# Reordering the waits of a two-block network kernel: loads, filters, attention norm, merges and norms

## What is computed

```python
# block 1
m = silu(c) @ w_ada + b_ada                       # shifts, scales, gates
h = rmsnorm(x) * (1 + sc1) + sh1;  z = h @ w_in + b_in
f = sin-MLP(t) @ f4 * decay                       # Hyena filters, 2 orders, fwd and bwd
f = f / sum(|f|)                                  # over time and direction
zc = short 3-tap convolution of z[:, :1536]; v, x1, x2 = split(zc)
for o in (0, 1): y = gate_o * (irfft(rfft(y) * rfft(f)[o]) + skip[o] * y)
q, k = rope(rmsnorm(z_q)), rope(rmsnorm(z_k))     # 8 heads of 64
na = softmax(q @ [k_window; rmsnorm(k_ctx)].T / 8 + bias) @ [v; v_ctx]
x += g1 * ((sig(z_g1) * (y @ w_hy_out) + sig(z_g2) * (na @ w_na_out)) @ w_out)
hf = rmsnorm(x) * (1 + sc2) + sh2
# PEER: 8 heads pick 16 of 16384 experts for each row by two-part keys
x += g2 * sum(softmax(best) * gelu(hf . u[idx]) * v[idx])
# block 2, two layers: attention and a state-space mixer (SSD) side by side,
h = rmsnorm(x);  merged = gates of (attention @ pa, y_ssd @ ps);  x += merged @ w_o
h = rmsnorm(x);  x += glu(conv(h @ w_up)) @ w_dn  # 22 column tiles
out = rmsnorm(x)
```

## Time and profile before

| | us |
|---|---|
| median of 3 runs (2389.24 to 2395.49) | 2389.31 |
| the profiled execution | 2386.79 |
| its span, first to last instruction | 2385.0 |
| TensorE busy (86%) | 2047.3 |
| VectorE (58%), ScalarE (42%), GpSimd (41%) | 1395.0, 994.6, 980.6 |

### The profile page before, as it was taken

How to read it: one execution, slowest core, us unless ns; L and a number is a source line. 1 busy time by engine, 2 the same in 40 slices (tenths; PEclk the granted TensorE clock), 3 DMA queues, 4 the chain that set the end, 5 groups by cost and what they waited for, 6 DMA issues and landing times.

```text
span 2385.0 us, 26693 instructions
## 1 busy us (share of the span) xinstructions
PE 2047.3 (86%) x9656; PEld 1505.9 (63%) x9656; DVE 1395.0 (58%) x2697; ACT 994.6 (42%) x1756; POOL 980.6 (41%) x562
## 2 busy tenths in 40 slices
PE   6898698778788777777799989989989988998998
PEld 1486467763333333333489777789978976777997
DVE  2785674466666676675336645257753673434776
ACT  1430334321212121211345677355554567744554
POOL 1162246554444444444377547610027844781000
PEclk9899799889989899899999999999989999998999
DMA  8141355459999999999655344445545533453552
GB/s 325 39 141 46 129 210 187 139 235 422 422 421 421 421 421 421 421 421 422 217 166 171 109 144 156 158 146 186 188 139 163 185 106 124 159 184 116 188 188 102
DMA packets 111012, 534.37 MB, mean 224 GB/s; under 512 B 12448, under 2 KB 12576, under 8 KB 77344
## 3 DMA queue, kind: packets, MB, share of 16 engines
q1 hardware_dynamic: 66960, 244.72, 31.1%
q0 software_dynamic: 38720, 275.96, 28.1%
q10 hardware_dynamic: 5200, 11.98, 1.6%
...
## 4 chain that ended last, share of the span: by engine, by line
PE 54%; DMA 24%; DVE 8%; ACT 7%; issue 4%; POOL 3%; ACTq 0%; DVEq 0%; SPq 0%; POOLq 0%
PE psum L791 53%; DMA pair_rows<-in_peer_uv,arena 10%; DMA arena<-in_peer_uv,arena 6%; DMA wring<-in_peer_uv,arena 5%; POOL w_lo L2369 2%; ACT w_hi L1251 2%; ACT arena L1262 1%; DVE arena L1619 1%; PE psum L839 1%; ACT arena L1510 1%; DMA wring<-in_w_ada 1%; ACT arena L1455 1%; DMA dve_junk<-acs_rows 1%; ACT a_hi L1258 1%; DVE dve_junk L1619 1%
## 5 line engine op out<-in xcount | busy, mean ns | idle before, releaser
L2369 POOL TENSOR_TENSOR w_lo<-wring,w_hi 128x1024 fp32r<-128x1024 f32 x282 | 697.9, 2489 | 729.7 <-ACT w_hi L1251 687.9
L1251 ACT ACTIVATE w_hi<-wring 128x1024 fp32r<-128x1024 f32 (+1 forms) x414 | 431.6, 1051 | 357.4 <-PE psum L791 311.7
L791 PE MATMUL psum<-w_hi,a_hi 128*128 128x512 f32 (+1 forms) x1056 | 425.1, 403 | 31.8 <-POOL w_lo L2369 20.7
L791 PE MATMUL psum<-w_lo,a_hi 128*128 128x512 f32 (+1 forms) x1056 | 415.5, 393 | 0.0
L791 PE MATMUL psum<-w_hi,a_lo 128*128 128x512 f32 (+1 forms) x1056 | 415.4, 393 | 0.0
L791 PE MATMUL psum<-arena 128*128 128x512 f32 (+7 forms) x1142 | 342.7, 458 | 81.9 <-ACT arena L1403 45.2
L791 PE MATMUL psum<-a_hi,w_hi 128*128 128x256 f32 x1312 | 377.7, 288 | 11.0 <-POOL w_lo L2369 3.8
L791 PE MATMUL psum<-a_lo,w_hi 128*128 128x256 f32 x1312 | 376.3, 287 | 0.0
L791 PE MATMUL psum<-a_hi,w_lo 128*128 128x256 f32 x1312 | 376.0, 287 | 0.0
L791 PEld LDWEIGHTS psum<-arena 128*128 128x128 f32 (+2 forms) x1142 | 186.5, 200 | 224.9 <-issue 159.0
L791 PE MATMUL psum<-pair_rows,arena 128*128 128x512 f32 x512 | 260.6, 663 | 67.3 <-ACT arena L1403 67.3
...
## 6 DMA issues: line engine op xcount, KB each, us to landing
wring<-in_w_up SPq DMA_DIRECT2D x88, 512.0 KB, 3.3
wring<-in_w_xbc SPq DMA_DIRECT2D x48, 512.0 KB, 3.3
wring<-in_w_dn SPq DMA_DIRECT2D x44, 512.0 KB, 3.3
wring<-in_w_adaT SPq DMA_DIRECT2D x32, 512.0 KB, 4.0
wring<-in_w_qkv SPq DMA_DIRECT2D x32, 512.0 KB, 3.5
wring<-in_w_z SPq DMA_DIRECT2D x32, 512.0 KB, 3.5
wring<-in_w_g SPq DMA_DIRECT2D x32, 512.0 KB, 3.4
wring<-in_w_ps SPq DMA_DIRECT2D x32, 512.0 KB, 3.3
```

The source lines that it names most:

```text
L791: mm = lambda o, a, b, start, stop: nc.tensor.matmul(o, a, b, start=start, stop=stop, skip_group_check=True)
L1251: a.reaches(A(w_hi[:, n % SPLIT_RING, 0:width], wring[:, c % RING, 0:width], ACT.Copy), hi_ready, n + 1)
L2369: nc.gpsimd.tensor_tensor(w_lo[:, r, 0:width], wring[:, c % RING, 0:width], w_hi[:, r, 0:width].bitcast(F32), ALU.subtract).then_inc(lo_re ...
```

## The change

1. **Loads in order of use.** The first four w_ada chunks go ahead of `consts`, x comes after all 16; on ScalarE's queue the first three filter matrices and `feats` go first, `f4` and the other tables after `ada(0)`; GpSimd loads the context after `ada` 1 is filled.
2. **Filters by order, their norm behind the DFT.** The filters of order 0 come first; sum and difference are made of filters that are not normalized; the sums follow the DFT, and VectorE multiplies the spectra by the reciprocal (`spectra_scaled`) during `zhy`. On ScalarE the norm of x and context comes ahead of the absolute values. The first `zhy` product waits for its inputs tile by tile.
3. **Short convolution from PSUM.** ScalarE takes the middle tap with scale and bias out of PSUM, VectorE adds the outer taps from PSUM.
4. **Attention norm.** Queries are normalized and rotated (in place, tables prepared early) behind order 0's spectrum products, keys behind order 1's; squares of projected rows are ScalarE's.
5. **Merge in halves.** `mT` is turned in two halves, the first ahead of the gate rows (block 2: in the middle of `ps` 2, 3), the second in the middle of `w_out` 0, 1 (`w_o` 0, 1). The eight late dots move from between `w_pq` chunks to `mix` and after `mT`.
6. **Norms by tile.** `norm_tiles` squares each half as its residual comes, with the root's table loaded ahead; scaling and output go by tile. The last two `dn` chunks are taken together in the order 0, 2, 1, 3. Transposed inputs are waited for singly (`ready`).
7. **GpSimd's low parts in two instructions** of half the width.

```diff
-    ada(3), add("filter", 8), g.append(("adaT", 3)), add("absum", 2)
+    ada(3), g.extend(("filter", i) for i in FILTER_ORDER), g.append(("adaT", 3))
     for o in range(2):
         g.extend([("dftf", 4 * o + i) for i in range(4)] + [("nyq", o)])
+    add("absum", 2)
     add("hT0", KD), add("hcT", KD)
     add("zhy", 12), add("zqkv", 2), add("vrow", 2)
     for o in range(2):
...
-    add("mix", 8), add("mT", KD), add("gb", 2), add("wout", 4)
-    add("hfT", KD), add("hfrow", 4), 
+    add("mix", 8), add("mT", 4), add("gb", 2), add("mT", 4, 4), add("wout", 4)
+    add("hfT", KD)
     for q in range(4):
-        g.extend([("pq", 4 * q + i) for i in range(4)] + [("ps", q)])
+        for i in range(4):
+            g.append(("pq", 4 * q + i))
+            if 4 * q + i == 0:
+                add("hfrow", 4)
...
+DOWN_ORDER = (0, 2, 1, 3)
+FILTER_ORDER = [4 * t + 2 * o + j for o in range(2) for t in range(TT) for j in range(2)]
 ADA_FIRST, ADA_DOTS, DOTS_PER_HEAD, LATE_DOTS = 4, 32, 3, 8
+LATE_AFTER = [("mix", 1), ("mix", 3), ("mix", 5), ("mix", 7)] + [("mT", KD - 1)] * 4
+LATE_AT = [2, 4, 6, 8, 9, 10, 11, 12]
...
+            if c == 4:
+                sp.dma_start(consts[:], d["consts"]).then_inc(S("consts_in"), 16)
+            if c == 4 * ADA_FIRST:
+                sp.dma_start(x[:], d["x"].rearrange("p (a b) -> p a b", b=D)).then_inc(S("x_in"), 16)
...
+        for i in FILTER_ORDER:
+            o = open_("filter", i)
+            t, j = i // 4, i % 4
+            close(mm(o, mlp_h[0:64, tile(t)], HW("f4")[0:64, j * 512:(j + 1) * 512], True, True))
         ada_columns(3)
...
-        pe.wait_ge(S("modulated_lo"), KD)
         for m_ in range(12):
-            feature_mm("w_in_hy", None, "zhy", m_)
+            feature_mm("w_in_hy", None, "zhy", m_, None if m_ else lambda k: pe.wait_ge(S("modulated_lo"), k + 1))
...
+        merged_turned("mT", merged, 0, 1)
         gate_rows("gb", 0, 1)
-        for c in range(2):
-            columns_of_rows("w_out", None, [("wout", 2 * c), ("wout", 2 * c + 1)], [0, 0])
-
-
-        pe.wait_ge(S("scaled"), 2)
+        columns_of_rows("w_out", None, [("wout", 0), ("wout", 1)], [0, 0], early=True,
+                        before=lambda: merged_turned("mT", merged, 1, 2), ready=lambda k: wait_read(pe, "mT", k))
...
+                feature_mm("w_pq", None, "pq", m_, None if m_ else lambda k: pe.wait_ge(S("modulated_lo"), 2 * KD + k + 1))
+                if m_ == 0:
+                    for t in range(TT):
+                        for half in range(2):
...
+            columns_of_rows("w2_ps", l, [(L + "ps", 0), (L + "ps", 1)], [0, 0], 8,
+                            ready=lambda k: wait_read(pe, L + "yT", k))
+            columns_of_rows("w2_ps", l, [(L + "ps", 2), (L + "ps", 3)], [0, 0], 8, early=True,
+                            before=lambda: merged_turned(L + "mT", merged2, 0, 3 + 2 * l))
+            columns_of_rows("w2_o", l, [(L + "wo", 0), (L + "wo", 1)], [0, 0], early=True,
+                            before=lambda: merged_turned(L + "mT", merged2, 1, 4 + 2 * l),
+                            ready=lambda k: wait_read(pe, L + "mT", k))
+            columns_of_rows("w2_o", l, [(L + "wo", 2), (L + "wo", 3)], [0, 0])
...
+                if c == FT // 2:
+                    pe.wait_ge(S("glu_ready"), FT * l + FT)
+                    last_two = [take("w2_dn", l), take("w2_dn", l)]
+                    for n in DOWN_ORDER:
+                        for k, w in zip((FT - 2, FT - 1), last_two):
+                            m = rows_mm(down[n], GLU_AT + k % GLU_RING, 1, n % 2, w, 512, False, k == FT - 1,
+                                        at=512 * (n // 2))
+                            if k == FT - 2 and n == 3:
+                                m.then_inc(weights_used, 1)
+                        close(m)
+                    break
                 for k in range(2 * c - 2, 2 * c) if c else ():
...
+        def norm_tiles(n, halves, ready):
+
+            a.done(A(lnw[:, 0:1], K("epscol"), ACT.Sqrt))
+            summed = []
+            for i in halves:
+                c, t = i // 2, i % 2
+                half = slice(512 * c, 512 * c + 512)
+                second = t in summed
+                ready(i)
+                part = ss[:, 2 + t:3 + t] if second else ss[:, t:t + 1]
+                a.done(A(xs[:, t, half], x[:, t, half], ACT.Square, accum_out=part))
+                a.settle()
+                if second:
+                    a.reaches(A(std[:, t:t + 1], part, ACT.Sqrt, scale=1.0 / D, bias=mean_half[:, t:t + 1]),
+                             S("tile_std"), 2 * n + t + 1)
+                else:
+                    a.done(A(mean_half[:, t:t + 1], part, ACT.Identity, scale=1.0 / D, bias=K("epscol")))
+                    summed.append(t)
+
...
+            a.reaches(A(zcT[:, m_, :], bank("zhy", m_)[:, 0:SEQ], ACT.Identity, bias=hy_bias[:, m_:m_ + 1],
+                        scale=V("cw", 12 + m_)), S("hy_first_tap"), m_ + 1)
...
+        def tiles_scaled(n):
+
+            for t in range(TT):
+                dve.wait_ge(S("tile_std"), 2 * n + t + 1)
+                v.done(T.reciprocal(rinv[:, t:t + 1], std[:, t:t + 1]))
+                v.settle()
+                v.reaches(T.tensor_scalar(xs[:, t, :], x[:, t, :], rinv[:, t:t + 1], None, ALU.mult),
+                         S("tile_scaled"), 2 * n + t + 1)
...
+        def spectra_scaled(o_):
+
+            wait_read(dve, "absum", o_)
+            v.done(T.reciprocal(rsum[:, o_, :], rsum[:, o_, :]))
+            v.settle()
+            for spectrum in (Kr[:, o_, :, :], Ki[:, o_, :, :]):
+                tt(spectrum, spectrum, rsum[:, o_:o_ + 1, :].to_broadcast([P, 2, 512]), ALU.mult)
+            tt(Kr0[:, o_, :], Kr0[:, o_, :], rsum[:, o_, :], ALU.mult)
...
+        filters_in(0)
+        even_and_odd(0)
+        filters_in(1)
+        ada_out(3)
+        even_and_odd(1)
+        absolutes(0)
+        absolutes(1)
...
+        def attention_queries():
+
+            dve.wait_ge(S("na_squares"), 2)
+            row_sums(na_sq, 0)
+            v.settle()
+            dve.sem_inc(S("na_sumsq"), 1)
+            roped_rows(0)
+            dve.wait_ge(S("na_std"), 1)
+            v.done(T.reciprocal(ninv[:, 0:16], nstd[:, 0:16]))
+            v.settle()
+            scaled_rows(qkv[:, :, 0:512], 0)
+            v.settle()
...
+            (attention_queries if o_ == 0 else attention_keys)()
...
+            late_dot("mix", n)
...
-                n = ADA_DOTS - LATE_DOTS + m_ // 2
-                ada_dots(n, n + 1)
...
-            nc.gpsimd.tensor_tensor(w_lo[:, r, 0:width], wring[:, c % RING, 0:width],
-                                    w_hi[:, r, 0:width].bitcast(F32), ALU.subtract).then_inc(lo_ready, 1)
+                pool.wait_ge(S("scaled"), 2)
+            half = width // 2
+            nc.gpsimd.tensor_tensor(w_lo[:, r, 0:half], wring[:, c % RING, 0:half],
+                                    w_hi[:, r, 0:half].bitcast(F32), ALU.subtract)
+            nc.gpsimd.tensor_tensor(w_lo[:, r, half:width], wring[:, c % RING, half:width],
```

523 lines of the change are left out of this document (284 added, 239 removed).

## The result

The changed kernel takes 2326.6 us (median of 4 runs, 2324.12 to 2328.98) against 2389.27 for the kernel before (4 runs, 2384.44 to 2395.49): ratio 0.974, 95% interval 0.972 to 0.976. It is faster by 62.7 us where 105 were forecast, and 2326.6 lies above the range of 2260 to 2312.

A forecast was written before the change was run, and what follows sets the result against it. TensorE was taken to bound the front and back parts, the DMA engines 507.33 to 1155 us. Terms of -75 up to the gather's start, -34 behind and +4 for halves made -105: 2284 us, range 2260 to 2312.

The forecast's parts named there:

- The attention and SSD sum: Attention and SSD stretches of two layers: +6.6 us, from +2.6 of the state-space part and all +4 of the halves.
- Merge and w_out: Merge to last w_out matmul: turning in halves removes a 4.4 us wait, moved dots delay two chunks; -0.6 us.
- Queries without dots: Query chunks up to the gather's first issue: without dots between them the gather starts at the last split; -20 us.
- The merge turned in halves: Each layer's merge behind the gather: turning in halves between chunks removes idle time and a low clock; -7 us per layer.
- Norm ahead of the FFN: In each layer, the 10.94 us norm stretch, of which TensorE works 3.69, shortens by 5 us.
- The tail: End of the kernel, 12.0 us with two full squares and a table load in it: -3.5 us.
- Loads -13: Kernel start: first w_ada chunk issued first lands at some 6 us instead of 19.4, other loads fit behind; -13.3 us.
- the loads are late: Rival, 8%: filter tables arrive late, decay products wait, 8 to 13 of the 13 us come back; 2292 to 2297.
- Filters -9.5, first projection -3.5: Filters ordered, norm behind the DFT: -9.5 us; first projection tile by tile, removing a 2.8 us wait and slow clock: -3.5.
- Halves +4: Every GpSimd low part in two instructions: extra launch shows only in GpSimd-paced places; +4 us (0 to +25).
- slower by halves: Rival, 3%: each extra GpSimd instruction costs 0.39 us beyond the 0.32 TensorE leaves free, making the kernel slower.
- the moved work meets GpSimd: Rival, 15%: keys late by 5, w_out late by 5, halves at +15; 2305 in the middle, 2314 at the far end.

The follow-up runs named there:

- e1: The changed kernel with each GpSimd low part as one instruction again instead of two halves: 2318.7 us, ratio 0.9708 to the kernel before.
- e2: The changed kernel with the eight late dots moved back between the query chunks: 2332.16 us, ratio 0.9767 to the kernel before.
- e4: The changed kernel with the first half of the merged rows turned after two ps chunks instead of four (second half likewise): 2315.35 us, ratio 0.9686.
- e5: The changed kernel with all 32 dots during the attention heads, four a head, none later: 2318.83 us, ratio 0.9739 to the kernel before.
- e9: e6 with x loaded four chunks later, the context after ada 3, and their waits behind the absolute values: 2323.93 us, ratio 0.9731.
- e11: e8 with the later x and context loads of e9: 2297.23 us, ratio 0.9619 to the kernel before.
- e12: e11 with low parts in halves in block 1 only, whole behind the gather: 2286.85 us, ratio 0.9596 to the kernel before.
- e3: The changed kernel with the twelve rotation-table products moved ahead of the short convolution: 2321.08 us, ratio 0.9731 to the kernel before.
- e6: e3 with ScalarE's norm of x and context also moved behind the absolute values: 2322.7 us, ratio 0.9733 to the kernel before.
- e7: The changed kernel with the edits of e4, e5 and e6 together: 2305.85 us, ratio 0.9665 to the kernel before.
- e8: e7 with each GpSimd low part as one whole instruction: 2300.01 us, ratio 0.9633 to the kernel before.
- e13: The kernel before with all dots in the attention heads, four a head, and low parts in halves: 2375.11 us, ratio 0.9949.

## Why the prediction was wrong

The direction and most mechanisms held: attention norm, second norm, the norm between the layers, and the first chunk at 5.99 us all within 0.5 us of their terms. The attention and SSD sum, +6.5 for +6.6, is luck: e1 with whole low parts has 375.0 there, the same as the kernel before, so the halves cost 6.5 of their own and the +2.6 booked beside them came to nothing. Of the signs that the prediction named, the first matmul at 6 us and the vanished wait at naT came, and the last w_pq split still releases the gather (0.28 us behind it); the DFT (51), the first score (213), the gather's start (432) and "no idle over 2 us at either mT" did not: 61, 226, 464 and 4.16.

The step that failed first is "Merge and w_out, -0.6 (-4 to +5)": +12.4, outside its own bounds. It named two mechanisms. The second, a read_low behind a dot, did not show: the 5.1 us wait for `a_lo` is ScalarE behind a late chunk. The first, a late slot, is the right one, but it was priced as two chunks once late by 2 to 4 us. ScalarE waited six times, 17.4 us in all, since a late slot delays the chunk whose product VectorE must read before the next dot; in the timelines the end of a dot releases SP's next load four times. And "Queries without dots, -20" (measured -17.4) was booked as a gain beside it, while e2 shows the two to be one cost in two places: -20.9 and +19.1. That is 13 of the 45 us.

**Behind the gather.** "The merge turned in halves -7" per layer gave -0.45 and -3.0. The wait did not go, it moved to ScalarE's order of work. This is 10.5 us of the miss, and e4 takes back 7.1 in layer 0 and 2.4 in layer 1 by one number. "Norm ahead of the FFN -5" gave -2.8 and -3.2, a term that was too large: TensorE's 3.7 us of transposes and the vector work ahead of them stayed. The tail gave -5.2 for -3.5.

**Loads -13** was right at its start (5.99) and gave 6.4 back before the filters (4.4 to 4.7 in e2, e4 and e5), the rival "the loads are late", which had 8%; what came late was w_ada itself, not the tables, and e9, e11 and e12 show x and the context to be the cause. The prediction's own figures said so: at 415 GB/s a stage of 7.9 us moves 3.3 MB, four chunks are 2.1 of them, and four such rooms of 1.2 MB hold 4.7 MB, not 6. The windows of the kernel before up to its filters, then the changed kernel's `ada` stages:

```profile
0.00:19.47 19.47, 0.00 (x0) 0.03 (x1) 0.00 (x0) 1.50 (x2) 0.90 (x5) 1.00 0.91 368
19.47:52.30 32.83, 32.83 (x82) 6.85 (x83) 8.27 (x23) 5.62 (x9) 4.05 (x2) 1.00 0.88 292
```

```profile
5.99:45.20 39.21, 35.47 (x83) 6.80 (x83) 8.86 (x27) 3.93 (x8) 2.02 (x3) 0.96 1.01 391
```

The DMA engines are full there. The first two rows make 16.8 MB, and the changed kernel moves 16.7 up to its filters (15.3 in its row, 1.4 ahead of it).

**Filters -9.5, first projection -3.5** gave -5.4 to the end of the convolutions (counted from the first filter to the first score, e2, e4 and e5 are another 1.3 to 2.5 us shorter). The sum had VectorE at 0.74 us for 512 columns and left out the twelve rotation products (9.16 us) that this change puts there. e3 and e6 take them away and get 1.5 to 3 us; in both the slow clock took up the stretch, in e7 it lay ahead of it (10.43 us), and in e9 one held product costs the same again. So the term had three covers, one over the other, and none of them was in the sum.

**Halves +4**: the whole cost is 8 us by e1's median and 6 by e7's and e8's (12 behind the gather, 8 of them given back in front), a term of the right kind. The rival "slower by halves" needed 0.39 us on each split beyond what was free; the extra is 0.26 in all. The argument beside it was one-sided. The Trainium skill ("SBUF — State Buffer", "Who interferes with whom") says that the one who comes second blocks for a whole instruction; the trace agrees in the heads (1.22, 2.32 and 3.39 us for one dot). In e9 a product was held through six halves in a row (7.25 us), longer than one instruction. I read it as two chances for VectorE to hold a split, and not as half the wait for VectorE, which is what e13 shows to be worth 8.5 us in the heads.

**The rival "the moved work meets GpSimd"** (15%, 2305 to 2314) comes nearest, but for the wrong place: the keys were not late; the dots were. Terms failed together in one direction (merge, layers, loads, filters), and the range had them as if each could fail alone.

What stays open: why the attention and SSD stretches vary by up to 6 us with halves and by 1.4 with whole low parts, why VectorE is held for six instructions in one place and for one in others, and what decides where the slow clock falls around the filters.
